# One step's order changed in the combine stage, and one product's order in the attention stage, of a two-layer decoder kernel

## The chip, the cores and the metric

The program runs on one core of one Trainium2 chip. The metric is the time of one execution on the device, in microseconds (us). Before the change it is 5105.31 us, the median of 3 runs (5102.03 to 5113.32).

## What is computed

4096 tokens, 1024 channels, in 32 blocks of 128 tokens. The reference is a decoder of two layers; cut to what matters here:

```
h   = x + pool_mixer(rmsnorm(x));  h += moe(rmsnorm(h))
h   = h + sigmoid(rmsnorm(h) @ w_ple_gate) * (p0 @ w_ple_up)
q   = rope(rmsnorm(h) @ w_q) / 8;  k = rope(rmsnorm(h) @ w_k);  v = rmsnorm(h) @ w_v
o   = attention of each 128 queries over the last 128 keys, with a sink per head
h   = h + o @ w_o;  h += moe(rmsnorm(h));  h += gated embedding p1
out = rmsnorm(h)
```

Two stages are touched. The combine stage of the first layer makes lines two and three: it adds the experts' two rows of a token, makes the gate, adds the embedding, and makes q, k and v, which it writes to HBM in the turned layout that attention reads. The attention stage makes lines four and the first half of five.

Large products are made in three bfloat16 parts: an operand is split into a high part (its bfloat16 rounding) and a low part (the rest), and high x high, high x low and low x high are summed in PSUM (`mm3`, lines 108 to 112: line 110, 111 and 112 in this order).

## The kernel before

The stages follow one another; each engine has its own instruction stream, written out by hand in a `step` function, and the streams meet at semaphores. SP issues the plain transfers and the transposing ones (`DMA_TRANSPOSE`), in program order; a wait in SP's stream holds back everything behind it.

**Combine stage** (`combine_phase`, line 1110). A step `s` works on three blocks: `head` prepares block s+1, `mid_` is the gate of block s, `tail` is q, k and v of block s-1. There are 32 blocks; step 1 is the first with a tail, step 31 the last with a gate, step 32 has the tail alone.

- TensorE (lines 1486 to 1513): 48 products with `wg` for the gate of block s (two halves of 24), then 48 with `wq` and 24 with `wkv` for block s-1. The gate reads `xT` (two buffers). The others read `x3T`, the turned third rows of block s-1, of which there is one buffer; they wait for `x3_turned`.
- VectorE (lines 1413 to 1475): h2 and the low part of x for block s+1; the residual for block s (lines 1443 and 1446) and the low part of `x3` (line 1457); then the rotation of q and k of block s-1 and the low parts of q, v and k (lines 1468, 1471, 1474). ScalarE makes the high parts (lines 1359, 1362, 1364); it writes `v_row` only when the stores of the block before have landed (`qkv_st`, line 1361).
- SP (lines 1223 to 1283), in a step with all parts: wait for `x3l_done` of block s-1 and for `kv_mm` of block s-2 (which frees `x3T`), turn `x3` into `x3T`; store q, k and v of block s-2 (`store_qkv`, which first waits for `qk_turned`); load `hin` and `p_in` of block s+2; turn `ph` and `x` of block s+1 into `pT` and `xT`; store h3 of block s, load `up_in`, store `pT`; and at the end of the step wait for `ql_done` and `kl_done` of block s-1 and turn q and k of block s-1. So x3 of block s, ready in step s, is turned at the start of step s+1, behind the turning of q and k of block s-1.

In the profile q's rows are named `cb_raw` (they share memory with a weight buffer), `x3` and `x` are both shown as `cb_x`, and all five PSUM tiles as `cb_ps_b`.

**Attention stage** (`attention_phase`, line 1762). A step `s` has eight turns c = 0 to 7, one per pair of heads. In turn c TensorE makes the scores of pair c+3 (from c = 5 on those of the next block), VectorE the masked maximum of that pair (`top`, line 2020) and the low part of the weights of pair c (`rests`, line 2037), ScalarE the exponentials (line 1961), GpSimd the high part of the weights (line 1938), and SP turns them (line 1886). Around them, on TensorE: at c = 0 and 1 the projection with `wo` of the first four pairs of block s-1, in two halves of 512 columns; at c = 2 the product of weights and values of the last four pairs (`weigh`); at c = 4 and 5 the projection of these four; at c = 6 `weigh` of the first four pairs of block s. The result of `weigh` becomes `oT`: the high part by ScalarE (`out_hi`, line 1968), the low part by VectorE (`out_lo`, line 2044). Before the projection TensorE waits for `ol_done`, the low part, at c = 0 and at c = 4. At c = 3 VectorE makes `out_lo` and then the low part of the router's rows (`hrow`, line 2088).

Of the kernel before, what the change touches and what calls it, by code (L numbers as in the profile page):

```python
# [28 lines left out]
P = 128  # L29
D = 1024  # L30
T = 4096
NT = T // P
KD = D // P
# [36 lines left out]
def wait(eng, sem, value):  # L70

    if isinstance(value, int) and value <= 0:
        return
    eng.wait_ge(sem, value)
# [1035 lines left out]
def combine_phase(nc, A, C, layer, rot):  # L1110
# [4 lines left out]
    with ExitStack() as stack:  # L1115
        m = Mem(nc, f"cb{layer}", stack)
# [15 lines left out]
        jobs += [([(A["w_q"][0], 0, D)], k, g_q, wq) for k in range(KD)]  # L1132
        jobs += [([(A["w_k"], 0, KVW), (A["w_v"], KVW, 2 * KVW)], k, g_kv, wkv) for k in range(KD)]
        GQ = KD + KD
        landed, count = [], [0] * RAW
        for n, job in enumerate(jobs):
            count[n % RAW] += 16 * len(job[0])
# [44 lines left out]
        def steps(eng, step, early=lambda: None):  # L1182

            step(-2, 0, True, False, False, False)
            early()
            step(-1, 1, True, True, False, False)
            step(0, 0, True, True, True, False)
            step(1, 1, True, True, True, True)
            with eng.Fori(1, NT // 2 - 1) as i:
                step(2 * i, 0, True, True, True, True)  # L1190
                step(2 * i + 1, 1, True, True, True, True)
            step(NT - 2, 0, False, True, True, True)
            step(NT - 1, 1, False, False, True, True)
            step(NT, 0, False, False, False, True)

        @block.sync
        def _(sp):
# [11 lines left out]
            def turn(dst, src, sem):  # L1209

                sp.dma_start(dst[:].rearrange("p h k n -> p (h k) n"), src[:].rearrange("p h d -> p (h d)"),
                             transpose=True).then_inc(sem, 16)

            def store_qkv(t):

                sp.wait_ge(qk_turned, 32 * t + 32)
                sp.sem_inc(turn_open, 1)
                at = slice(t, t + 1) if isinstance(t, int) else bass.ds(t, 1)
                for rows, src in ((C.qT_rows, q_turned), (C.kT_rows, k_turned[:].rearrange("p j n -> p (j n)")),
                                  (C.v_rows, v_row[:].rearrange("p h n -> p (h n)"))):  # L1220
                    sp.dma_start(rows[at].rearrange("o p n -> (o p) n"), src).then_inc(qkv_st, 16)

            def step(s, u, load, head, mid_, tail):
                v = 1 - u
                if tail:
                    t = s - 1
                    sp.wait_ge(x3l_done, t + 1)
                    sp.sem_inc(turn_open, 1)
                    if not (isinstance(t, int) and t == 0):
                        sp.wait_ge(kv_mm, t)  # L1230
                        sp.sem_inc(turn_open, 1)
                    turn(x3T, x3, x3_turned)
                    if not (isinstance(t, int) and t == 0):
                        store_qkv(t - 1)
                if load:
                    t = s + 2
                    wait(sp, h2_done, t - 1)
# [24 lines left out]
                if mid_:  # L1262
                    sp.wait_ge(h3_done, 2 * s + 2)
                    sp.dma_start(h3_t[s], h3[u][:]).then_inc(h3_st[u], 16)
                    if load:
# [3 lines left out]
                    at = slice(s, s + 1) if isinstance(s, int) else bass.ds(s, 1)  # L1269
                    sp.dma_start(C.pT_rows[at].rearrange("o p n -> (o p) n"),  # L1270
                                 pT[u][:].rearrange("p h k n -> p (h k n)")).then_inc(pT_st[u], 16)
                if tail:
                    t = s - 1
                    sp.wait_ge(ql_done, t + 1)
                    sp.sem_inc(turn_open, 1)
                    sp.wait_ge(kl_done, t + 1)
                    sp.sem_inc(turn_open, 1)
                    wait(sp, qkv_st, 48 * t)
                    sp.sem_inc(turn_open, 1)
                    sp.dma_start(q_turned.rearrange("p (n m) -> p n m", m=P), q_row.rearrange("p n two e -> p (n two e)"),  # L1280
                                 transpose=True).then_inc(qk_turned, 16)
                    sp.dma_start(k_turned[:], k_row[:].rearrange("p j a b e -> p (j a b e)"),
                                 transpose=True).then_inc(qk_turned, 16)

            steps(sp, step)
            store_qkv(NT - 1)
            sp.wait_ge(qkv_st, 48 * NT)
            for u in (0, 1):
                sp.wait_ge(h3_st[u], 8 * NT)
                sp.wait_ge(pT_st[u], 8 * NT)  # L1290
# [26 lines left out]
        def _(act):  # L1317
# [11 lines left out]
            def step(s, u, load, head, mid_, tail):  # L1329
# [25 lines left out]
                if tail:  # L1355
                    t = s - 1
                    act.wait_ge(rot_add, 3 * t + 2)
                    wait(act, qk_turned, 32 * t)
                    act.activation(q_row[:, :, 0, :], q_out[:].rearrange("p (n e) -> p n e", e=HEAD), ACT.Copy).then_inc(qh_done, 1)
                    act.wait_ge(rot_mul, 3 * t + 3)  # L1360
                    wait(act, qkv_st, 48 * t)
                    act.activation(v_row[:, 0, :], ps_kv[:, KVW:2 * KVW], ACT.Copy).then_inc(vh_done, 1)
                    act.wait_ge(rot_add, 3 * t + 3)
                    act.activation(k_row[:, :, 0, :, :], k_out[:].rearrange("p (j e) -> p j e", e=HEAD).unsqueeze(2).to_broadcast([P, NKV, 2, HEAD]),
                                   ACT.Copy).then_inc(kh_done, 1)
# [396 lines left out]
def attention_phase(nc, A, C):  # L1762
# [8 lines left out]
    with ExitStack() as stack:  # L1771
# [233 lines left out]
        def _(dve):  # L2005
# [53 lines left out]
            def step(s, r, load, nxt, cur, prev, prev2):  # L2059
                u = r % 2  # L2060
                v = 1 - u
                for c in range(NP):
# [11 lines left out]
                    if c == 1 and prev2:  # L2074
                        if isinstance(s, int) and s == 2:
# [2 lines left out]
                        wait(dve, hnT_mm, s - 2)  # L2078
                        dve.scalar_tensor_tensor(out=hn[:], in0=h4[u][:], scalar=rs[:, 0:1], in1=g_ffn[:],
                                                 op0=ALU.mult, op1=ALU.mult).then_inc(hn_done, 1)  # L2080
                    if c == 3 and prev:
                        out_lo(s - 1, 1)
                    if c == 4 and isinstance(s, int) and s == -1:
                        sinks()
                    if c == 3 and prev2:
                        dve.wait_ge(hi_done, s - 1)
                        dve.wait_ge(hn_done, s - 1)
                        dve.tensor_tensor(hrow[u][:, D:2 * D], hn[:], hrow[u][:, 0:D], ALU.subtract).then_inc(lo_done, 1)
                    if c in (5, 6) and prev:
                        residual(s - 1, v, c - 5)  # L2090
                    if c < NP - 3 and cur:
# [14 lines left out]
        def _(pe):  # L2106
# [27 lines left out]
                                       start=n == 0, stop=n == len(products) - 1)  # L2134
                mm.then_inc(pv_mm, 1)

            def project(n, jj):

                c = slice(512 * n, 512 * n + 512)
                for k in range(HALF * jj, HALF * jj + HALF):  # L2140
                    mm = mm3(pe, ps_x[:, c], oT[:, 0, k, :], oT[:, 1, k, :], wo[:, 0, k, c], wo[:, 1, k, c],
                             k == 0, k == KD - 1)
                return mm

            def step(s, r, load, nxt, cur, prev, prev2):
                u = r % 2
                v = 1 - u
                for c in range(NP):
                    if c < NP - 3 and cur:
                        scores(s, r, c + 3)  # L2150
                    if c == 5 and prev:
                        project(1, 1).then_inc(wo_mm, 1)
                    if c >= NP - 3 and nxt:
                        scores(s + 1, (r + 1) % KR, c + 3 - NP)
                    if c == 0 and prev:
                        if isinstance(s, int) and s == 1:
                            pe.wait_ge(w_lo_done, HALF)
                        pe.wait_ge(ol_done, 2 * s - 1)
                        wait(pe, h4_done, 2 * (s - 1))
                        project(0, 0)  # L2160
                    if c == 1 and prev:
                        project(1, 0)
                    if c == 2 and prev:
                        weigh(s - 1, (r - 1) % KR, 1)
                    if c == 3 and prev2:
# [5 lines left out]
                    if c == 4 and prev:  # L2171
                        if isinstance(s, int) and s == 1:
                            pe.wait_ge(w_lo_done, NP)
                        pe.wait_ge(ol_done, 2 * s)
                        project(0, 1).then_inc(wo_mm, 1)
                    if c == 6 and cur:
                        weigh(s, r, 0)
                    if c == 7 and prev2:
# [85 lines left out]
```

## Time and profile before

| | |
|---|---|
| median of 3 runs | 5105.31 us |
| the profiled execution | 5107.4 us, span 5105.7 us |
| TensorE matmul | 4546.8 us busy, 89% of the span |
| VectorE | 2893.9 us busy, 57% |
| ScalarE | 2044.3 us busy, 40% |
| GpSimd | 1606.1 us busy, 31% |
| TensorE clock granted, mean | 0.952 of full speed |
| combine stage, steady part | about 1680 to 2535 us of the span |
| attention stage, steady part | about 2615 to 3390 us |

Busy shares are means over the whole span; the two stages together are some 1,800 us of it. [...] A matmul of 512 columns has a record of 0.38 us at the upper level, and the next one starts 0.216 us after it; at the lower level the record has 0.63 us.

### The profile page before, as it was taken

The page shows a single profiled execution, that of the slowest core. Times are in us where ns is not written, and L with a number is a line of the kernel's source. Part 1 is how long each engine was busy: PE and PEld are TensorE (multiplying, and loading weights), DVE is VectorE, ACT ScalarE, POOL GpSimd, SP SyncE. Part 2 cuts the span into 40 slices and gives each one's busy share as a digit, 9 for nine tenths or more (in the row PEclk, how much of TensorE's full clock was granted, in tenths as well). Part 3 has the DMA queues.
Part 4 walks back from the last instruction along what each step waited for, and adds up shares of the span by engine and source line. Part 5 has one row for each costly group of instructions (what it writes and reads, how often), then busy time and mean ns, then how long its engine had stood idle before and what let it go on. Part 6 is the DMA issues. An engine that isn't in the chain of part 4 may idle for free. (4 is left out here: it accounts for less than half of the span.)

```text
span 5105.7 us, 93235 instructions
## 1 busy us (share of the span) xinstructions
PE 4546.8 (89%) x29795; PEld 2864.6 (56%) x30217; DVE 2893.9 (57%) x5879; ACT 2044.3 (40%) x2994; POOL 1606.1 (31%) x1161
## 2 busy tenths in 40 slices
PE   7986999999995899999858888886999999997999
PEld 6954776666672344444335555543676767665444
DVE  6774444444444555555468888874444444443676
ACT  6844444343432222232235454544443443331443
POOL 1104444443440111111023333422444444431332
PEclk9997999999997999999979999988999999999999
DMA  8968899898876778788677777766898889885664
GB/s 246 320 222 289 279 307 276 270 292 283 266 249 193 191 201 204 203 204 203 150 173 184 185 191 192 187 175 247 272 293 291 275 284 299 273 259 169 243 233 169
DMA packets 1262631, 1204.87 MB, mean 236 GB/s; under 512 B 925857, under 2 KB 961697, under 8 KB 1262497
## 3 DMA queue, kind: packets, MB, share of 16 engines
q1 hardware_dynamic: 1216416, 1069.05, 71.2%
q0 software_dynamic: 46080, 134.27, 8.3%
q8 instruction: 56, 0.92, 0.1%
q14 instruction: 79, 0.64, 0.0%
HBM read 742.77 MB, written 274.73 MB: 199 GB/s over the span
## 5 line engine op out<-in xcount | busy, mean ns | idle before, releaser
L837 POOL TENSOR_TENSOR ex_w_lo<-ex_raw,ex_w_hi 128x2048 bf16<-128x2048 f32 x192 | 780.6, 4090 | 1103.1 <-ACT ex_w_hi L896 1102.9
L896 ACT ACTIVATE ex_w_hi<-ex_raw 128x2048 bf16<-128x2048 f32 x384 | 707.0, 1900 | 385.8 <-PE ex_ps_y L112 189.4
L1008 PE MATMUL ex_ps_gate<-ex_xT,ex_w_hi 128*128 128x0 bf16 x2048 | 566.8, 277 | 140.1 <-DMA ex_xT<-ex_xrow 89.0
L1009 PE MATMUL ex_ps_gate<-ex_xT,ex_w_hi 128*128 128x0 bf16 x2048 | 566.7, 277 | 0.0
L1010 PE MATMUL ex_ps_gate<-ex_xT,ex_w_lo 128*128 128x0 bf16 x2048 | 566.4, 277 | 0.0
L1008 PE MATMUL ex_ps_up<-ex_xT,ex_w_hi 128*128 128x0 bf16 x2048 | 558.8, 273 | 0.0
L1009 PE MATMUL ex_ps_up<-ex_xT,ex_w_hi 128*128 128x0 bf16 x2048 | 558.6, 273 | 0.0
L1010 PE MATMUL ex_ps_up<-ex_xT,ex_w_lo 128*128 128x0 bf16 x2048 | 558.5, 273 | 0.0
L988 DVE COPY ex_y<-ex_ps_y 128x512 f32 x324 | 224.1, 692 | 566.7 <-PE ex_ps_y L112 564.4
L972 DVE TENSOR_TENSOR ex_aT<-ex_silu,ex_ps_up 128x384 bf16<-128x384 f32 x256 | 141.8, 554 | 682.8 <-PE ex_ps_up L1010 502.5
L111 PE MATMUL ex_ps_y<-ex_w_lo,ex_aT 128*128 128x512 bf16 x1296 | 492.1, 380 | 8.5
L112 PE MATMUL ex_ps_y<-ex_w_hi,ex_aT 128*128 128x512 bf16 x1296 | 491.9, 380 | 0.0
L907 ACT ACTIVATE ex_silu<-ex_ps_gate 128x384 f32<-128x384 f32 x256 | 124.8, 489 | 866.5 <-PE ex_ps_gate L1010 866.1
L1938 POOL TENSOR_TENSOR att_pr<-att_ex,att_rden 128x512 bf16<-128x512 f32 x256 | 294.1, 1149 | 489.6 <-DVE att_rden L2030 484.3
L837 DVE TENSOR_TENSOR ex_w_lo<-ex_raw,ex_w_hi 128x2048 bf16<-128x2048 f32 x192 | 439.9, 2293 | 14.3 <-ACT ex_w_hi L896 14.3
L110 PE MATMUL ex_ps_y<-ex_w_hi,ex_aT 128*128 128x512 bf16 x1134 | 431.3, 380 | 6.5 <-DVE ex_aT L976 6.5
L1961 ACT ACTIVATE att_ex<-att_score,att_nmx 128x257 f32<-128x257 f32 x512 | 256.2, 502 | 395.8 <-DVE att_nmx L2025 395.8
L111 PE MATMUL att_ps_x<-att_wo,att_oT 128*128 128x512 bf16 x512 | 218.3, 426 | 105.1 <-DVE att_oT L2044 105.1
L1008 PEld LDWEIGHTS ex_ps_gate<-ex_xT,ex_w_hi 128*128 128x128 bf16 x2048 | 203.1, 99 | 177.6 <-issue 122.5
L110 PE MATMUL cb_ps_b<-cb_wq,cb_x3T 128*128 128x512 bf16 x510 | 198.4, 389 | 79.5 <-DMA cb_x3T<-cb_x 79.4
L2020 DVE CUSTOM_DVE_ANT_0 att_score<-att_ps_s,all_mask,att_sink 128x256 f32<-128x256 f32 x496 | 218.2, 477 | 69.6 <-PE att_ps_s L2118 69.6
L110 PE MATMUL cb_ps_b<-cb_wg,cb_xT 128*128 128x512 bf16 x511 | 195.3, 382 | 60.7 <-DMA cb_xT<-cb_x 43.5
(350 smaller groups left out, 9491.2 us busy)
## 6 DMA issues: line engine op xcount, KB each, us to landing
ex_raw<-in_w_exp_gate SPq DMA_DIRECT2D x128, 1024.0 KB, 9.4
ex_raw<-in_w_exp_up SPq DMA_DIRECT2D x128, 1024.0 KB, 11.7
ex_raw<-in_w_exp_down SPq DMA_DIRECT2D x128, 1024.0 KB, 5.9
y_rows<-ex_y SPq DMA_DIRECT2D x162, 512.0 KB, 3.0
up_rows<-rt_up_out SPq DMA_DIRECT2D x64, 512.0 KB, 2.6
cb_hin<-h_mid SPq DMA_DIRECT2D x64, 512.0 KB, 3.9
cb_up_in<-up_rows SPq DMA_DIRECT2D x64, 512.0 KB, 4.5
mix_x<-in_x SPq DMA_DIRECT2D x32, 512.0 KB, 5.2
```

The lines of the kernel that those rows point to most:

```text
L110: pe.matmul(out, lhs_hi, rhs_hi, start=first, stop=False)
L111: pe.matmul(out, lhs_hi, rhs_lo, start=False, stop=False)
L112: return pe.matmul(out, lhs_lo, rhs_hi, start=False, stop=last)
L837: eng.tensor_tensor(w_lo[u][:, w], raw[:, c, :], w_hi[u][:, w], ALU.subtract).then_inc(lo_done, 1)
L896: act.activation(w_hi[u][:, c * WCHUNK:(c + 1) * WCHUNK], raw[:, c, :], ACT.Copy).then_inc(hi_done, 1)
L988: dve.tensor_copy(y[:, bass.ds(j, 1), 512 * n:512 * n + 512].rearrange("p o d -> p (o d)"), ps_y[n][:]).then_inc(y_done, 1)
L1008: pe.matmul(out, hi, x_hi, start=j == 0, stop=False)
L1009: pe.matmul(out, hi, x_lo, start=False, stop=False)
L1010: mm = pe.matmul(out, lo, x_hi, start=False, stop=j == KD - 1)
L1938: pool.tensor_tensor(pr[c % ER][:, 0, :, :], ex[c % ER][:, :, 0:W], rden[:, 2 * c:2 * c + 2].unsqueeze(2).to_broadcast([P, 2, W]), ALU.mul ...
L1961: e = act.activation(ex[c % ER][:, k, :], score[c][:, k, :], ACT.Exp, bias=nmx[:, n:n + 1], accum_out=esum[:, n:n + 1])
L2020: last = dve.tensor_tensor_reduce(out=score[c][:, k, 0:W], in0=ps_s[:, c % 2, k, :], in1=mask[:], scale=1.0, scalar=sink[:, head(c, k):hea ...
```

## The change

In the combine stage SP turns q and k of block s-2 at the start of step s, behind `x3T`, where the step before it had turned them at its end; the stores of q, k and v of block s-2 move from the start of step s to its end. `qkv_st` starts at 48, so that waits on it have positive values from the first block on. In the attention stage the projection makes all products with the high part of `oT` first, and waits for the low part only then; `out_lo` and the low part of `hrow` change places on VectorE at c = 3.

```diff
@@ combine_phase
+        QKV = 3 * 16
@@ sync
+            def turn_qk(t):
+                sp.wait_ge(ql_done, t + 1)
+                sp.sem_inc(turn_open, 1)
+                sp.wait_ge(kl_done, t + 1)
+                sp.sem_inc(turn_open, 1)
+                sp.wait_ge(qkv_st, QKV * t + QKV)
+                sp.sem_inc(turn_open, 1)
+                sp.dma_start(q_turned.rearrange("p (n m) -> p n m", m=P), q_row.rearrange("p n two e -> p (n two e)"),
+                             transpose=True).then_inc(qk_turned, 16)
+                sp.dma_start(k_turned[:], k_row[:].rearrange("p j a b e -> p (j a b e)"),
+                             transpose=True).then_inc(qk_turned, 16)
@@ step of SP
                     turn(x3T, x3, x3_turned)
                     if not (isinstance(t, int) and t == 0):
-                        store_qkv(t - 1)
+                        turn_qk(t - 1)
...
-                if tail:
-                    t = s - 1
-                    sp.wait_ge(ql_done, t + 1)
-                    sp.sem_inc(turn_open, 1)
-                    sp.wait_ge(kl_done, t + 1)
-                    sp.sem_inc(turn_open, 1)
-                    wait(sp, qkv_st, 48 * t)
-                    sp.sem_inc(turn_open, 1)
...
+                if mid_ and tail and not (isinstance(s, int) and s == 1):
+                    store_qkv(s - 2)
+
+            sp.sem_inc(qkv_st, QKV)
             steps(sp, step)
+            store_qkv(NT - 2)
+            turn_qk(NT - 1)
             store_qkv(NT - 1)
-            sp.wait_ge(qkv_st, 48 * NT)
+            sp.wait_ge(qkv_st, QKV * NT + QKV)
@@ step of ScalarE
-                    wait(act, qkv_st, 48 * t)
+                    act.wait_ge(qkv_st, QKV * t + QKV)
@@ attention_phase, step of VectorE
-                    if c == 3 and prev:
-                        out_lo(s - 1, 1)
...
                     if c == 3 and prev2:
                         dve.wait_ge(hi_done, s - 1)
                         dve.wait_ge(hn_done, s - 1)
                         dve.tensor_tensor(hrow[u][:, D:2 * D], hn[:], hrow[u][:, 0:D], ALU.subtract).then_inc(lo_done, 1)
+                    if c == 3 and prev:
+                        out_lo(s - 1, 1)
@@ TensorE
-            def project(n, jj):
+            def project(t, n, jj):
 
                 c = slice(512 * n, 512 * n + 512)
-                for k in range(HALF * jj, HALF * jj + HALF):
-                    mm = mm3(pe, ps_x[:, c], oT[:, 0, k, :], oT[:, 1, k, :], wo[:, 0, k, c], wo[:, 1, k, c],
-                             k == 0, k == KD - 1)
+                ks = range(HALF * jj, HALF * jj + HALF)
+                pe.wait_ge(oh_done, 2 * t + jj + 1)
+                for k in ks:
+                    for part in (0, 1):
+                        pe.matmul(ps_x[:, c], oT[:, 0, k, :], wo[:, part, k, c], start=k == 0 and part == 0, stop=False)
+                pe.wait_ge(ol_done, 2 * t + jj + 1)
+                for k in ks:
+                    mm = pe.matmul(ps_x[:, c], oT[:, 1, k, :], wo[:, 0, k, c], start=False, stop=k == KD - 1)
                 return mm
@@ step of TensorE
-                        pe.wait_ge(ol_done, 2 * s - 1)
                         wait(pe, h4_done, 2 * (s - 1))
-                        project(0, 0)
+                        project(s - 1, 0, 0)
...
-                        pe.wait_ge(ol_done, 2 * s)
-                        project(0, 1).then_inc(wo_mm, 1)
+                        project(s - 1, 0, 1).then_inc(wo_mm, 1)
```

## Rows read from the trace of the kernel before

**Rows 1.** Waits, whole kernel: engine line <- releaser: us, times, longest

```profile
PE att_ps_x L111 <- DVE att_oT L2044: 105.1, 63, 4.0
...
PE cb_ps_b L110 <- DMA cb_x3T<-cb_x: 79.4, 31, 11.9
```

**Rows 2.** Groups by line, PE, whole kernel: xcount | busy us, mean ns | idle

```profile
L111 PE MATMUL att_ps_x<-att_wo,att_oT 128*128 128x512 bf16 x512 | 218.3, 426 | 105.1 <-DVE att_oT L2044 105.1
...
L112 PE MATMUL cb_ps_b<-cb_wq,cb_x3T 128*128 128x512 bf16 x511 | 198.7, 389 | 1.7 <-issue 0.2
...
L110 PE MATMUL att_ps_x<-att_wo,att_oT 128*128 128x512 bf16 x448 | 188.9, 422 | 0.4 <-DVE att_oT L2044 0.4
```

**Rows 3.** Waits, PE, combine alone, 1700 to 2480 us

```profile
PE cb_ps_b L110 <- DMA cb_x3T<-cb_x: 53.8, 27, 2.4
```

**Rows 4.** Timeline, PE, combine: start us, us, line, op [idle before <-releaser]

```profile
2055.14 0.38 PE L110 MATMUL cb_ps_b<-cb_wg,cb_xT 128*128 128x512 bf16 x1
...
2065.29 0.38 PE L112 MATMUL cb_ps_b<-cb_wg,cb_xT 128*128 128x512 bf16 x1
2067.51 0.39 PE L110 MATMUL cb_ps_b<-cb_wq,cb_x3T 128*128 128x512 bf16 x1 [1.85 <-DMA cb_x3T<-cb_x]
...
2083.06 0.38 PE L110 MATMUL cb_ps_b<-cb_wg,cb_xT 128*128 128x512 bf16 x1
...
2544.81 0.61 PE L110 MATMUL cb_ps_b<-cb_wq,cb_x3T 128*128 128x512 bf16 x1 [11.91 <-DMA cb_x3T<-cb_x]
```

**Rows 5.** Timeline, SP's queue, the same combine step

```profile
2059.03 1.76 SPq L1280 DMA_TRANSPOSE cb_raw<-cb_raw  x1
...
2063.05 2.09 SPq L1211 DMA_TRANSPOSE cb_x3T<-cb_x  x1
...
2074.94 0.58 SPq L1270 DMA_DIRECT2D pT_rows<-cb_pT  x1
```

**Rows 6.** DMA issues, combine, 1700 to 2480 us: last number is us to landing

```profile
qT_rows<-cb_raw SPq DMA_DIRECT2D x27, 512.0 KB, 3.2
...
cb_x3T<-cb_x SPq DMA_TRANSPOSE x27, 4.4
```

**Rows 7.** Timeline, DVE and ACT, the same combine step

```profile
2056.28 0.38 ACT L1362 ACTIVATE cb_v_row<-cb_ps_b 128x256 bf16<-128x256 f32 x1 [2.80 <-DVE cb_rab L1400]
...
2058.08 0.68 DVE L1474 TENSOR_TENSOR cb_k_row<-cb_k_out,cb_k_row 128x512 bf16<-128x512 f32 x1
...
2071.80 1.28 DVE L1457 SCALAR_TENSOR_TENSOR cb_x<-cb_h,cb_rs,cb_x 128x1024 bf16<-128x1024 f32 x1 [1.84 <-ACT cb_x L1354]
```

**Rows 8.** Stretches, combine: us, PE, PEld, DVE, ACT, POOL busy, PEclk, DMA share

```profile
2057.00:2059.00 2.00, 2.00 (x11) 0.88 (x9) 2.00 (x4) 0.66 (x2) 0.00 (x0) 1.00 0.00 0
...
1700.00:2480.00 780.00, 722.46 (x3238) 323.27 (x3305) 436.87 (x801) 219.74 (x328) 88.69 (x134) 0.99 0.80 202
```

**Rows 9.** Timeline, PE, attention: one step's two waits, and the last step's

```profile
3050.98 0.38 PE L111 MATMUL att_ps_x<-att_wo,att_oT 128*128 128x512 bf16 x1 [0.65 <-DVE att_oT L2044]
...
3063.47 0.63 PE L111 MATMUL att_ps_x<-att_wo,att_oT 128*128 128x512 bf16 x1 [2.29 <-DVE att_oT L2044]
...
3378.11 0.38 PE L111 MATMUL att_ps_x<-att_wo,att_oT 128*128 128x512 bf16 x1 [1.39 <-DVE att_oT L2044]
```

**Rows 10.** Timeline, ACT, DVE and POOL, the same attention step

```profile
3042.34 2.00 POOL L1938 TENSOR_TENSOR att_pr<-att_ex,att_rden 128x512 bf16<-128x512 f32 x1 [0.56 <-DVE att_rden L2030]
...
3049.39 1.03 POOL L1938 TENSOR_TENSOR att_pr<-att_ex,att_rden 128x512 bf16<-128x512 f32 x1 [2.08 <-DVE att_rden L2030]
...
3061.45 0.57 ACT L1968 ACTIVATE att_oT<-att_ps_o 128x512 bf16<-128x512 f32 x1
...
3062.33 0.68 DVE L2044 TENSOR_TENSOR att_oT<-att_ps_o,att_oT 128x512 bf16<-128x512 f32 x1
```

**Rows 11.** Stretches, attention: a usual step, and one over a loop boundary

```profile
3039.65:3063.47 23.82, 20.89 (x159) 12.49 (x161) 20.49 (x74) 12.50 (x40) 9.75 (x9) 0.93 0.81 191
2790.39:2817.93 27.54, 22.53 (x159) 12.84 (x161) 21.10 (x74) 12.31 (x40) 9.75 (x9) 0.87 0.75 180
```

More of the change, by code:

```diff
@@ L1271, in step @@
                                  pT[u][:].rearrange("p h k n -> p (h k n)")).then_inc(pT_st[u], 16)
-                if tail:
-                    t = s - 1
-                    sp.wait_ge(ql_done, t + 1)
-                    sp.sem_inc(turn_open, 1)
-                    sp.wait_ge(kl_done, t + 1)
-                    sp.sem_inc(turn_open, 1)
-                    wait(sp, qkv_st, 48 * t)
-                    sp.sem_inc(turn_open, 1)
[L1280 to L1283, printed above, removed]
+                if mid_ and tail and not (isinstance(s, int) and s == 1):
+                    store_qkv(s - 2)
+            sp.sem_inc(qkv_st, QKV)
             steps(sp, step)
+            store_qkv(NT - 2)
+            turn_qk(NT - 1)
             store_qkv(NT - 1)
-            sp.wait_ge(qkv_st, 48 * NT)
+            sp.wait_ge(qkv_st, QKV * NT + QKV)
             for u in (0, 1):
@@ L2151, in step @@
                     if c == 5 and prev:
-                        project(1, 1).then_inc(wo_mm, 1)
+                        project(s - 1, 1, 1).then_inc(wo_mm, 1)
                     if c >= NP - 3 and nxt:
@@ L2157, in step @@
                             pe.wait_ge(w_lo_done, HALF)
-                        pe.wait_ge(ol_done, 2 * s - 1)
                         wait(pe, h4_done, 2 * (s - 1))
-                        project(0, 0)
+                        project(s - 1, 0, 0)
                     if c == 1 and prev:
-                        project(1, 0)
+                        project(s - 1, 1, 0)
                     if c == 2 and prev:
```

## The prediction

> **What bounds the kernel now.** I read the waits of the whole kernel first, to see whether the change touches anything that TensorE waits for. TensorE is the busiest engine, and of its waits the two largest outside the expert stage are the two that the diff is about [rows 1]: 105.1 us for the low part of `oT` in attention, 63 times, and 79.4 us for `x3T` in combine, 31 times, one of them 11.9 us long. Then the groups by line, for what a wait costs beyond itself [rows 2]: the projection's products last 426 and 422 ns on average and those with `wq` 389, where an undisturbed one lasts 380 and one at half clock 630. So some products behind the waits run at the lower clock. Last the timelines of one step of each stage.
>
> **Combine, why x3T is late.** In the steady stretch TensorE waits for `x3T` 27 times, 53.8 us together and never over 2.4 [rows 3], so 2.0 each, once per step, and for nothing else. Take the step whose gate starts at 2055.14 and call that zero; the products of k and v of the block before have just ended. The gate's last product starts at +10.15, the first `wq` product at +12.37, and the next gate at +27.92 [rows 4]. The 2.22 between the first two is one spacing of 0.216 and 2.0 of wait. SP starts turning q at +3.9, then k, and `x3T` only at +7.9 [rows 5]; with 4.4 to landing [rows 6] that is +12.3, when TensorE resumes. What SP waited for is the low part of k on VectorE, which ends at +3.6 (2058.08 + 0.68), while the low part of x3 for the next turn is ready at +17.9 (2071.80 + 1.28) [rows 7], ten microseconds before the end of the step. So x3T's rows are ready early, and stand behind q and k in SP's queue.
>
> **Combine after the change.** What must precede the turning of `x3T` is now x3 (ready at +17.9 of the step before) and the last product that reads the old `x3T`, which ends at zero. SP reacts 0.27 after its releaser (2058.76 to 2059.03), so the turning starts at about +0.3 and lands at +4.7, by 4.4 to landing [rows 6], against +10.4, when TensorE wants it: the wait goes, with 5.7 to spare. The DMA engines stand idle at about that point of the step, in the stretch from 2057 [rows 8]. q and k still go at about +3.9, since their rows aren't ready earlier: SP is done with `x3T` by then, because that instruction holds its queue some 2.1. All that follows in the queue (`hin`, `p_in`, `pT`, `xT`) moves up by about 3, having neither the 2 us of `x3T` nor the three stores in front of it, so `xT` isn't late next. The stores of q, k and v go behind the store of `pT`, which SP issues at +19.8 [rows 5] and would at about +17: they are issued by +19.5. Covered is this by the rest of the step: they must have landed before ScalarE rewrites `v_row`, which it does 1.1 after the products of k and v end [rows 7], at +27, and before q is turned at +29.8. Landing after 3.2 [rows 6] leaves 4; the cover gone, ScalarE would hold k's rows and SP, and with 10 us more the next gate. The first `sem_inc` costs nothing that can be measured.
>
> Price: the step falls from 27.9 to 25.9, the length of its 120 products. Each wait of 1.99 [rows 3] gives back 2.15, as 1.85 of shown wait went with 2.00 of gap in the step above; 30 steps, 64. The clock: `wq` products at 389 for 380 ns, out of the 250 that lie between the levels, are 4% of 1536 or 55 at half clock, 0.216 each, 12; of these I take 10, as the first and the last step keep theirs. The last tail (11.91 of wait [rows 4]) keeps 4.7 of it: 7. **Sum 81.** Bounds: 60, if a part of the waits stays, and 85.
>
> **Attention.** In a usual step TensorE waits 0.65 ahead of the last four pairs' projection and 2.29 ahead of the first four pairs' [rows 9]. Both begin in the trace with a product of line 111, where the code has line 110 first: that record is missing, so the true waits are some 0.4 and 2.0. ScalarE's high part ends at 3062.02, VectorE's low part at 3063.01 [rows 10]. Starting with the high products saves at most the 0.99 between these, and at the other place the whole 0.4. The eight high products last 1.73, longer than 0.99, so the wait for the low part is covered. At c = 3 `out_lo` now comes after a subtraction of 1024 columns, about 1.2 later at worst by the like one on x3 (1.28 [rows 7]); that too is within 1.73, and VectorE fills with it the time in which it stood waiting for ScalarE. Waits that the diff adds: one on `oh_done`, which is what the low part waited for before.
>
> The clock is the larger part. [...] By the means (424 against 380, 18% of 1536 products, 0.216 each) this costs 58 over the stage, 1.8 per step. The wait that I leave is about 1.0, nearer the two that kept the clock, and I take the whole 58. [...]
>
> TensorE alone would then need 23.82 - 1.0 - 0.4 - 1.8 = 20.6 per step, but VectorE is busy 20.49 of these 23.82 [rows 11]: from here on it binds too. The two wait for each other (VectorE for scores queued behind projections, TensorE for `oT`), so neither floor is reached; I leave VectorE 0.9 of its 3.3 idle and take 21.4. A step over a loop boundary has 27.54 [rows 11]; I give it the same 2.4. 31 steps: **75**. Bounds: 31 (1 per step, VectorE keeps most of its waits) and 99 (3.2, the floors).
>
> **A row on a port.** GpSimd's product for the weights lasts 1.03, but 2.00 where VectorE starts an operation of 1024 columns on SBUF just before it (the rows at 3049.39 and 3042.34) [rows 10]. The swap at c = 3 puts `hrow`'s subtraction in this place: right behind the reciprocal that releases GpSimd. About 2.9 of VectorE's work lies between that and its use of the product, so I price it at nothing; at worst it is 1 per step.
>
> [...]
>
> **Sum.** 81 + 75 = 156 from the profiled execution of 5107.4: 4951, which stood 2 over the median, so 4950.
>
> **Rivals.**
> 1. *The clock still falls in attention* (12%). For it: it falls after every wait of about 2.3. Against: not after 1.39. The step would be 23.82 - 1.4 = 22.4: 44 instead of 75, 4981.
> 2. *The DMA engines bind combine* (6%). They are busy 0.80 of the step [rows 8], 22.3 us, which would be 0.86 of 25.9, and the stores now fall together with h3's and the gathers. If half the gain goes: 4990. Against: a landing may be 5.7 late.
> 3. *The port* (5%): 1 per step, 31 less, 4981.
> 4. *VectorE binds attention at once* (9%): step at 22.8, 31 saved, 4994.
> 5. *The floors are reached in attention* (10%): 20.6, 99 saved, 4926.
> 6. *Slower* (3%): the stores at the step's end land late, ScalarE stands at `v_row`, and behind it k's rows, SP's turning, `xT` and the gate. It decides from landings at about +33 (6 us of slack in `xT`) and loses time in all beyond +35, as each step then waits over the 2.15 given back; at +38, 30 steps lose 3: 90 - 75 = 15 slower, 5120. Against: 3.2 to landing now.
>
> **How the numbers follow.** 55% for the forecast. The range takes in its bounds and rivals 1 to 4: 4925 to 5000. About 0.2% (10 us) is what can be told from no change. Faster 0.95; same 0.02 (combine's gain lost in part and attention's too); slower 0.03.
>
> **What would show it.** Right: no wait on `x3T` in the steady stretch, gates 25.9 apart, x3T's turning ahead of q's by some 3.6 and landing in 4 to 6; in attention steps of about 21.4, line 111's place as the waiting product taken by a high one with about 1.0, mean records of the projection near 385, VectorE over 90% busy. Wrong: a new wait on `xT`, on `v_row` or on the low part of `oT`; projection records still at 0.63; GpSimd's product at 2.00 twice a step with VectorE waiting for it.

## The result, and the profile after

The changed kernel takes 4955.36 us, the median of 4 runs (4944.96 to 4959.94), against 5106.05 of the kernel before (4 runs, 5102.03 to 5113.32): a ratio of 0.97, 95% interval 0.9682 to 0.9719, 151 us less. The forecast was 4950. The profiled execution has a span of 4954.3.

First the waits of TensorE. Below are the wait on `oT` in the whole kernel, then the groups of the products that follow it, and the group with `wq` in combine:

```profile
PE att_ps_x L2151 <- ACT att_oT L1975: 53.0, 53, 1.6
```

```profile
L2151 PE MATMUL att_ps_x<-att_wo,att_oT 128*128 128x512 bf16 x960 | 245.9, 401 | 56.9 <-ACT att_oT L1975 53.0 <-DVE att_wo L2064 3.3
...
L112 PE MATMUL cb_ps_b<-cb_wq,cb_x3T 128*128 128x512 bf16 x511 | 195.2, 382 | 1.5
...
L2154 PE MATMUL att_ps_x<-att_wo,att_oT 128*128 128x512 bf16 x512 | 136.2, 390 | 0.0
```

Against [rows 1] the wait is now for ScalarE's high part (line 1975), not for VectorE's low part, and half as long; line 2154, the products with the low part, waits for nothing. Line 2151 has 960 records where the code makes 1024 products: as in [rows 9], the record of the first product behind each of the two waits of a step is missing, and each wait is shown 0.22 too long, in all some 11 of the 53. Against [rows 2] the `wq` products are down from 389 to 382 ns, near the 380 of undisturbed ones, and the projection's from 426 and 422 to 401 and 390: not down to 380. The clock still falls in some steps.

One step of combine, on TensorE and on SP's queue:

```profile
1989.26 0.38 PE L110 MATMUL cb_ps_b<-cb_wg,cb_xT 128*128 128x512 bf16 x1
...
1999.41 0.38 PE L112 MATMUL cb_ps_b<-cb_wg,cb_xT 128*128 128x512 bf16 x1
1999.62 0.38 PE L110 MATMUL cb_ps_b<-cb_wq,cb_x3T 128*128 128x512 bf16 x1
...
2015.16 0.38 PE L110 MATMUL cb_ps_b<-cb_wg,cb_xT 128*128 128x512 bf16 x1
```

```profile
1981.82 0.33 SPq L1235 DMA_DIRECT2D v_rows<-cb_v_row  x1
1989.53 1.93 SPq L1212 DMA_TRANSPOSE cb_x3T<-cb_x  x1
1993.15 1.74 SPq L1223 DMA_TRANSPOSE cb_raw<-cb_raw  x1
...
2001.78 1.85 SPq L1212 DMA_TRANSPOSE cb_xT<-cb_x  x1
```

The gates are 25.90 apart (27.92 in [rows 4]), and the first `wq` product follows the gate's last by 0.21, one spacing. The turning of `x3T` starts 0.27 after the products that read it have ended (+7.9 in [rows 5]), that of q 3.89 after, as before. In the stretch from 1700 to 2400 us TensorE shows no wait at all.

What became of the three stores at the end of the step is seen in the DMA landings of that stretch (last number, us) and on ScalarE:

```profile
qT_rows<-cb_raw SPq DMA_DIRECT2D x27, 512.0 KB, 7.2
...
v_rows<-cb_v_row SPq DMA_DIRECT2D x27, 128.0 KB, 8.6
...
cb_x3T<-cb_x SPq DMA_TRANSPOSE x27, 4.3
```

```profile
1990.48 0.38 ACT L1369 ACTIVATE cb_v_row<-cb_ps_b 128x256 bf16<-128x256 f32 x1 [2.88 <-DMA v_rows<-cb_v_row]
```

q's store lands after 7.2 where it took 3.2 [rows 6], and v's after 8.6. The kernel before already had a store at this place in the queue, and it was as slow (1700 to 2480 us):

```profile
pT_rows<-cb_pT SPq DMA_DIRECT2D x28, 128.0 KB, 8.1
```

ScalarE now waits for that landing (64.3 us in 22 waits) in most steps, but starts 1.22 after the products of k and v end, where it started 1.14 after [rows 7].

Attention. First the stretches (columns as in [rows 11]): a usual step, one with a fallen clock, and the steady stretch of combine. Then the same usual step on its engines:

```profile
2919.72:2940.92 21.20, 19.52 (x159) 12.10 (x161) 20.45 (x74) 12.47 (x39) 10.56 (x10) 1.00 0.86 214
...
2603.72:2626.19 22.47, 21.21 (x159) 12.52 (x161) 20.48 (x74) 12.50 (x39) 10.64 (x10) 0.92 0.88 212
1700.00:2400.00 700.00, 696.42 (x3177) 317.31 (x3244) 427.36 (x786) 216.21 (x324) 87.00 (x132) 1.00 0.84 223
```

```profile
2928.66 0.57 ACT L1975 ACTIVATE att_oT<-att_ps_o 128x512 bf16<-128x512 f32 x1
...
2929.52 1.67 PE L2151 MATMUL att_ps_x<-att_wo,att_oT 128*128 128x512 bf16 x7 [0.49 <-ACT att_oT L1975]
...
2934.48 1.06 PE L2125 MATMUL att_ps_s<-att_kT,att_qT 128*128 128x128 bf16 x16
...
2935.32 0.48 DVE L2027 CUSTOM_DVE_ANT_0 att_score<-att_ps_s,all_mask,att_sink 128x256 f32<-128x256 f32 x1 [0.44 <-PE att_ps_s L2125]
...
2940.92 1.67 PE L2151 MATMUL att_ps_x<-att_wo,att_oT 128*128 128x512 bf16 x7 [1.20 <-ACT att_oT L1975]
```

A usual step has 21.20 us for 23.82, with VectorE busy in 20.45 of them: its only wait is the 0.44 for the scores that stand behind the projection. TensorE keeps two waits, shown as 1.20 at c = 0 and 0.49 at c = 4. Both groups have seven of their eight products; less 0.22 for the missing first one, the waits are 0.98 and 0.27. The run with attention alone changed (below) has all eight in its profile and shows the same wait, once with the clock fallen behind it and once not:

```profile
2905.67 3.42 PE L2144 MATMUL att_ps_x<-att_wo,att_oT 128*128 128x512 bf16 x8 [0.98 <-ACT att_oT L1968]
...
2928.12 1.89 PE L2144 MATMUL att_ps_x<-att_wo,att_oT 128*128 128x512 bf16 x8 [0.99 <-ACT att_oT L1968]
```

Taken from one router sum (line 2107) to the next, 8 of the 31 steps have 22.4, and 5 at a loop's boundary 24.9 to 27.2 (27.4 to 27.7 before). The boundary steps differ by the clock: the two of 24.9 and 25.0 ran at 1.00 and 0.99 of full speed, the three of 26.7, 26.7 and 27.2 at 0.94, 0.88 and 0.94. Two of them:

```profile
2691.50:2716.50 25.00, 19.92 (x160) 11.98 (x160) 20.70 (x73) 12.45 (x40) 10.56 (x9) 1.00 0.73 183
2781.30:2808.00 26.70, 21.49 (x159) 12.35 (x160) 20.69 (x73) 12.34 (x39) 10.56 (x9) 0.94 0.78 175
```

On GpSimd the product beside the moved subtraction has 1.85, as the row at 3042.34 in [rows 10] had 2.00:

```profile
2926.57 1.04 POOL L1945 TENSOR_TENSOR att_pr<-att_ex,att_rden 128x512 bf16<-128x512 f32 x1 [1.07 <-DVE att_rden L2037]
2928.76 1.85 POOL L1945 TENSOR_TENSOR att_pr<-att_ex,att_rden 128x512 bf16<-128x512 f32 x1 [1.16 <-DVE att_rden L2037]
```

### The profile page after: what moved, and what is told of

It reads as the page before. It is cut to its first block and busy times, and to the rows that moved or that the text cites. A ratio compares the mean times of both kernels' runs of the same rounds, so it can differ in the third digit from the quotient of the medians.

```text
span 4954.3 us, 93219 instructions
## 1 busy us (share of the span) xinstructions
PE 4502.6 (91%) x29795; PEld 2854.9 (58%) x30217; DVE 2891.0 (58%) x5879; ACT 2043.1 (41%) x2994; POOL 1631.1 (33%) x1161
## 5 line engine op out<-in xcount | busy, mean ns | idle before, releaser
L1945 POOL TENSOR_TENSOR att_pr<-att_ex,att_rden 128x512 bf16<-128x512 f32 x256 | 319.3, 1247 | 400.6 <-DVE att_rden L2037 387.8
L2151 PE MATMUL att_ps_x<-att_wo,att_oT 128*128 128x512 bf16 x960 | 245.9, 401 | 56.9 <-ACT att_oT L1975 53.0
L931 POOL DMA_INDIRECT ex_xrow<-hn_rows,ex_token x192 | 204.0, 1063 | 98.9 <-POOL ex_token L926 57.6
L2044 DVE SCALAR_TENSOR_TENSOR att_pr<-att_ex,att_rden,att_pr 128x256 bf16<-128x256 f32 x512 | 224.2, 478 | 20.2 <-issue 18.1
```

The costliest lines, as they stand in the source:

```text
L1945: pool.tensor_tensor(pr[c % ER][:, 0, :, :], ex[c % ER][:, :, 0:W], rden[:, 2 * c:2 * c + 2].unsqueeze(2).to_broadcast([P, 2, W]), ALU.mul ...
L2151: pe.matmul(ps_x[:, c], oT[:, 0, k, :], wo[:, part, k, c], start=k == 0 and part == 0, stop=False)
```

## The experiments

All are timed beside the kernel before, whose medians in the four sessions were 5104.73, 5102.48, 5103.68 and 5101.58.

**The parts by themselves.** *Combine alone*: `combine_phase` of the changed kernel, all else of the kernel before.

> Combine changed, attention as before. My account: the two parts are separate stages and add up; 82 us of the 151 are combine's (gates 25.9 apart instead of 27.9 to 30.1), so about 5024. Rival: part of the attention gain comes from combine (earlier stores, another state of clock at its start); then this gives more or less than 82 and the two parts alone don't add up to 151.

5024.96 (ratio 0.984, 0.9824 to 0.9857), 79.8 less. *Attention alone*, the other way round.

> Attention changed, combine as before. My account: 65 us less, about 5041, steps of 21.2 with some of 22.4. Rival as for the run with combine alone: the parts don't add up, and this gives under 50 or over 80.

5032.76 (0.9856, 0.9838 to 0.9874), 72.0 less. Together 151.8, against 150.7 for the changed kernel: the parts add up, and the rival (one stage lives from the other) falls. Five steps had 22.4 here, eight in the changed kernel. At 1.25 each this is 4 us, well within the 15 by which the runs of this kernel differ (5025.68 to 5040.38).

**Attention's two edits.** *Without the swap*, on the changed kernel:

```diff
@@ VectorE, c == 3
+                    if c == 3 and prev:
+                        out_lo(s - 1, 1)
...
                         dve.tensor_tensor(hrow[u][:, D:2 * D], hn[:], hrow[u][:, 0:D], ALU.subtract).then_inc(lo_done, 1)
-                    if c == 3 and prev:
-                        out_lo(s - 1, 1)
```

> The changed kernel without VectorE's swap at c = 3. My account: VectorE binds attention, and without the swap it stands about 0.5 to 0.8 us per step waiting for ScalarE's high part, so steps of 21.8 and 15 to 25 us more than the changed kernel, about 4975. Rival: the high products first carry the whole gain and the swap is worth nothing, 4955. Rival of the port: the swap costs, because the subtraction falls beside GpSimd's product; then this is faster than 4950.

4970.99 (0.9729, 0.971 to 0.9748), 16 more than the changed kernel; their runs don't overlap, by 2 us. Usual steps have 21.44, and 10 steps have about 22.5, with the clock fallen. VectorE's waits between 2620 and 3240 us:

```profile
DVE att_pr L2044 <- issue: 21.3, 5, 4.6
DVE att_oT L2051 <- ACT att_oT L1975: 20.5, 28, 0.9
DVE att_score L2027 <- PE att_ps_s L2125: 12.3, 11, 1.4
```

The wait for ScalarE's high part, 0.7 a step, is what the swap fills. Only 0.24 of it comes out at the step, since the waits for scores shrink (12.3 for 26.3 us in the same stretch of the changed kernel). In the profiles the 23 usual steps give 7 of the difference (5 by the 0.24, 2 by two falls more of the clock) and the five boundary steps 2. The rest lies outside the steps, and runs of one kernel differ by as much.

*The swap alone*, on the kernel with combine changed.

```diff
@@ VectorE, c == 3
-                    if c == 3 and prev:
-                        out_lo(s - 1, 1)
...
                         dve.tensor_tensor(hrow[u][:, D:2 * D], hn[:], hrow[u][:, 0:D], ALU.subtract).then_inc(lo_done, 1)
+                    if c == 3 and prev:
+                        out_lo(s - 1, 1)
```

> Combine changed, attention with VectorE's swap alone, the projection still waiting for the low part in one piece. My account: the low part comes up to 0.5 us later at c = 4, TensorE waits for it in full there and waits 0.65 plus that, so attention is the same or a little slower than before: 5020 to 5035, against 5024 with combine alone. Rival: VectorE's own time binds already, and filling its wait gains 10 to 20 us by itself, 5005 to 5015.

5021.43, against 5024.96 with combine alone; their runs overlap (5019.93 to 5030.31 and 5024.06 to 5028.87). The steps have 24.0 in place of 23.85, the boundary steps 26.9 (one 25.2) in place of 27.3 to 27.8. Without the high products first the swap is worth nothing that can be told: VectorE doesn't bind while TensorE waits for the whole of `oT`.

**Which move counts in combine.** *q and k turned ahead of x3T*, in the new place; the stores stay at the end.

```diff
@@ step of SP, tail
+                    if not (isinstance(t, int) and t == 0):
+                        turn_qk(t - 1)
                     sp.wait_ge(x3l_done, t + 1)
...
                     turn(x3T, x3, x3_turned)
-                    if not (isinstance(t, int) and t == 0):
-                        turn_qk(t - 1)
```

> The changed kernel, but q and k turned ahead of x3T at the start of the step; the stores stay at its end. My account: only the place of x3T ahead of the other two counts, so the wait of 2.0 per step before the products with wq comes back with its fallen clock: about 75 more than the changed kernel, 5030, gates some 27.9 apart. Rival: the gain comes from the stores having moved (they no longer stand between x3T and pT), and this keeps most of it, under 4980.

5039.97 (0.9873, 0.9854 to 0.9892), 85 more than the changed kernel: all of combine's gain is gone (with attention alone changed it was 5032.76). TensorE's wait, and SP's queue:

```profile
PE cb_ps_b L110 <- DMA cb_x3T<-cb_x: 75.1, 32, 12.0
```

```profile
2003.44 1.95 SPq L1223 DMA_TRANSPOSE cb_raw<-cb_raw  x1
2005.43 1.72 SPq L1225 DMA_TRANSPOSE cb_k_turned<-cb_k_row  x1
2007.44 1.88 SPq L1212 DMA_TRANSPOSE cb_x3T<-cb_x  x1
```

`x3T` goes 4.0 after q, as in [rows 5], and the wait is back, with the last one of 12.0. Moving the stores gives nothing by itself.

*v stored at once*, behind the turning of q and k, on a semaphore of its own.

```diff
-        QKV = 3 * 16
+        QKV = 2 * 16
...
@@ turn_qk
+                sp.dma_start(C.v_rows[at].rearrange("o p n -> (o p) n"), v_row[:].rearrange("p h n -> p (h n)")).then_inc(v_st, 16)
@@ store_qkv
-                for rows, src in ((C.qT_rows, q_turned), (C.kT_rows, k_turned[:].rearrange("p j n -> p (j n)")),
-                                  (C.v_rows, v_row[:].rearrange("p h n -> p (h n)"))):
+                for rows, src in ((C.qT_rows, q_turned), (C.kT_rows, k_turned[:].rearrange("p j n -> p (j n)"))):
...
@@ step of ScalarE
-                    act.wait_ge(qkv_st, QKV * t + QKV)
+                    wait(act, v_st, 16 * t)
```

> The changed kernel with v stored right behind the turning of q and k, on a semaphore of its own, in place of the step's end. In the changed kernel ScalarE waits 64 us in all for the landing of v. My account: that wait is off the path (TensorE has no gap at all in the steady stretch), so it vanishes from the profile and the time stays, 4950 to 4960. Rival: it is on the path in some form (it holds k's rows and so the queue); then 20 us or more go.

4960.67 (4957.73 to 4963.06; 0.9721, 0.9705 to 0.9736): no gain. ScalarE's wait for v's landing is gone from the profile:

```profile
ACT cb_v_row L1372 <- DVE cb_rab L1410: 74.4, 27, 2.8
```

It waits for VectorE instead, for as long: 74.4 us, where the changed kernel had 64.3 for the landing and 14.0 for VectorE. The 64 us cost nothing that the time shows.

**What the remaining wait costs in clock.** *Four products more* ahead of the first projection; the projection overwrites their sum.

```diff
@@ project
+                if n == 0 and jj == 0:
+                    for k in range(4):
+                        pe.matmul(ps_x[:, c], wo[:, 0, k, 0:P], wo[:, 0, k, 0:512], start=k == 0, stop=k == 3)
```

> The changed kernel with four products of 512 columns more per attention step, ahead of the first projection, whose sum the projection overwrites; they fill 0.86 of the 1.2 us in which TensorE waits there. My account: this wait makes the clock fall in about a third of the steps, which costs 1.25 each, so with it filled all steps take 21.2 and 8 to 12 us go, about 4945, though more products are made. Rival: the clock falls for the idle time in the whole step or for the place in time; then the steps of 22.4 stay and nothing is gained. Or the fill delays: 25 us slower.

4948.03 (4941.22 to 4954.46; 0.9697, 0.9682 to 0.9712). None of the 31 steps has 22.4; the usual step is 21.20 as before. The time alone would not tell it from the changed kernel, the steps do. So the falls of the clock hang on TensorE's idle time at c = 0, the 0.98. TensorE has the 0.86 of these products to spare in every step: it doesn't bind.

**Taking the wait away.** *The high part ahead of the exponentials at c = 6*:

```diff
@@ step of ScalarE
+                    if c == 6 and cur:
+                        out_hi(s, 0)
                     if c >= NP - 3 and nxt:
                         exps(s + 1, c + 3 - NP)
...
-                    if c == 6 and cur:
-                        out_hi(s, 0)
```

> The changed kernel with ScalarE's high part of oT ahead of the exponentials of pair 1 at c = 6, so that it is there before TensorE asks. My account: TensorE's wait of 1.2 goes and the clock no longer falls, but VectorE is busy 20.5 of 21.2 us and binds: steps of 20.7 to 20.9, 20 to 25 us less, about 4933. Rival: VectorE doesn't bind, the step falls by the whole wait to 20.0, 45 us less, 4910. Second rival: the exponentials come later and hold VectorE, no gain.

4944.74 (4943.22 to 4948.62; 0.9692, 0.9679 to 0.9706). The clock no longer falls in any usual step (in one boundary step, of 27.0, it does), but the step stands at 21.20, not at 20.7 to 20.9 as my account had it. TensorE's waits and VectorE's between 2600 and 3160 us:

```profile
PE att_ps_x L2151 <- ACT att_oT L1975: 28.6, 25, 1.4
```

```profile
DVE att_score L2027 <- PE att_ps_s L2125: 13.3, 26, 2.1
```

The wait went from c = 0 to c = 4, and VectorE's 0.5 for the scores behind the projection stayed. A usual wait at c = 4, with all eight products behind it:

```profile
2657.75 1.90 PE L2151 MATMUL att_ps_x<-att_wo,att_oT 128*128 128x512 bf16 x8 [1.07 <-ACT att_oT L1975]
```

These 1.07 are longer than the 0.98 at c = 0 that let the clock fall in 8 steps, and here no usual step has a fall. So the length of the wait alone does not decide whether the clock falls. What else does, no run shows. The next run does the same *at c = 2 as well*:

```diff
@@ step of ScalarE
+                    if c == 2 and prev:
+                        out_hi(s - 1, 1)
                     if c < NP - 3 and cur:
                         exps(s, c + 3)
...
-                    if c == 2 and prev:
-                        out_hi(s - 1, 1)
```

> The kernel with ScalarE's high part ahead at c = 6, and now at c = 2 as well. Both that kernel and the one with the fill stood at 21.20 per step, with TensorE's wait at c = 4 (0.5 to 1.1) and VectorE's wait of 0.5 for the scores behind the projection. My account: these two are one ring (pair 5's maximum on VectorE, its exponentials, the high part, the projection, the scores, VectorE), and with the high part ahead at c = 2 the ring opens: VectorE never waits, steps of 20.7 to 20.8, 10 to 14 us less than with c = 6 alone, about 4932. Rival: VectorE's own time is 21.2 with all that its records don't show; then nothing changes, 4945.

4934.06 (4926.69 to 4935.28; 0.9669, 0.9654 to 0.9684), with steps of 20.66. All that VectorE still waits for between 2600 and 3160 us:

```profile
DVE att_pr L2044 <- issue: 20.2, 5, 4.5
```

The five are at the loop's boundaries. So 21.20 was a ring of engines that wait for each other in turn: pair 5's maximum, its exponentials, the high part behind them on ScalarE, the two projections, the scores behind these, VectorE.

**VectorE's own time.** *The low part of hrow on GpSimd*, on the changed kernel:

```diff
@@ VectorE, ahead of hn
+                        wait(dve, lo_done, s - 2)
@@ VectorE, c == 3
-                        dve.tensor_tensor(hrow[u][:, D:2 * D], hn[:], hrow[u][:, 0:D], ALU.subtract).then_inc(lo_done, 1)
...
@@ GpSimd
+                    if c == 3 and prev2:
+                        pool.wait_ge(hi_done, s - 1)
+                        pool.tensor_tensor(hrow[u][:, D:2 * D], hn[:], hrow[u][:, 0:D], ALU.subtract).then_inc(lo_done, 1)
```

> The changed kernel with the low part of hrow made by GpSimd in place of VectorE, 1.2 us per step less on VectorE. If VectorE's time is what holds the step at 21.2: 20 to 35 us less, 4920 to 4935. If it is the ring through the high part of oT at c = 4 alone: VectorE stands 1 us longer for ScalarE or for scores and nothing is gained, 4950 to 4960. Third: GpSimd is late with the weights and holds VectorE, slower than 4960.

4964.46 (4961.94 to 4965.66; 0.9729, 0.9712 to 0.9746), 9 more than the changed kernel, with steps of 21.25: nothing is gained, and the ratios' intervals overlap. GpSimd and VectorE at that place:

```profile
2912.09 2.13 POOL L1957 TENSOR_TENSOR att_hrow<-att_hn,att_hrow 128x1024 bf16<-128x1024 f32 x1
```

```profile
2911.61 0.69 DVE L2055 TENSOR_TENSOR att_oT<-att_ps_o,att_oT 128x512 bf16<-128x512 f32 x1 [0.68 <-ACT att_oT L1979]
...
2913.14 1.11 DVE L2036 TENSOR_SCALAR att_nmx<-att_mx 128x2 f32<-128x2 f32 x1
```

VectorE loses the 1.2 again: 0.68 waiting for ScalarE, and 0.94 in an instruction of two elements per partition, the negation of a maximum. It takes 0.17 elsewhere and here ends with GpSimd's, at 2914.2. *Both high parts ahead and the rows on GpSimd*:

> Both of the above together. My account: VectorE has 19.3 of work per step, TensorE about 19.6 without waits, so steps near 20.0 and 35 to 40 us less than the changed kernel, about 4918. Rival: GpSimd's longer work takes it back, 4930 or more.

4953.53 (4943.82 to 4958.81; 0.9703, 0.9686 to 0.972), 19 worse than without the rows on GpSimd, with steps of 21.24 and no wait on VectorE but those at the boundaries. The rival holds, and its size can be read:

```profile
2728.45 2.13 POOL L1957 TENSOR_TENSOR att_hrow<-att_hn,att_hrow 128x1024 bf16<-128x1024 f32 x1
```

```profile
2728.72 1.89 DVE L2036 TENSOR_SCALAR att_nmx<-att_mx 128x2 f32<-128x2 f32 x1
```

The negation takes 1.89, 1.72 more than 0.17, and ends with GpSimd's subtraction. VectorE is freed of 1.12 (its own subtraction, to the start of what followed): 20.66 - 1.12 + 1.72 = 21.26, and the step has 21.24.

*Both high parts ahead, and the negation on ScalarE*:

```diff
@@ top, VectorE
-                dve.wait_ge(mx_done, pairs(t, c))
-                dve.tensor_scalar(nmx[:, 2 * c:2 * c + 2], mx[:, 2 * c:2 * c + 2], -1.0, None, ALU.mult).then_inc(nmx_done, 1)
@@ exps, ScalarE
+                act.wait_ge(mx_done, pairs(t, c))
+                act.activation(nmx[:, 2 * c:2 * c + 2], mx[:, 2 * c:2 * c + 2], ACT.Copy, scale=-1.0).then_inc(nmx_done, 1)
```

> The kernel with both high parts ahead, and the negation of each pair's maximum (line 2032, 2 elements, 0.17 to 0.40 us each on VectorE, 8 per step) made by ScalarE in place of VectorE. In that kernel VectorE waits for nothing and the step is 20.66, so my account: VectorE's time alone holds it; 2.0 us less on VectorE bring the step down to TensorE's 19.6 to 20.0, 20 to 30 us less, about 4908. It also takes VectorE's one instruction that stood 1.1 us behind GpSimd's long one in the run with the rows on GpSimd. Rival: ScalarE's fixed cost comes into the ring from maximum to exponentials, TensorE and VectorE wait for it, and nothing or less than 10 us is gained.

4898.82 (4896.03 to 4903.92; 0.9602, 0.9589 to 0.9615): 57 less than the changed kernel, 35 less than the one that it is built on (20 to 30 were expected), with steps of 19.75. The stretch from 2600 to 3160 us of the changed kernel, and of this one:

```profile
2600.00:3160.00 560.00, 504.93 (x3921) 304.74 (x3970) 509.29 (x1792) 310.39 (x948) 263.14 (x224) 0.97 0.85 205
```

```profile
2600.00:3160.00 560.00, 543.75 (x4371) 333.61 (x4427) 517.13 (x1773) 385.08 (x1274) 286.85 (x249) 1.00 0.97 227
```

TensorE is up from 90% to 97%, with 1.00 of the clock granted for 0.97. Of the rival's fixed cost this much is seen: ScalarE's negation of two elements has 0.20, where its exponentials of 257 columns have 0.50. This is the best version found. Its gain has two halves. The 23 usual steps give 17 us (19.75 for 20.66), and the five boundary steps another 17: they have 21.3 to 21.8 where the kernel that it is built on has 24.5 to 25.4. The stall that VectorE had there, 20.2 us in 5 above, is down to this:

```profile
DVE att_score L2029 <- issue: 0.9, 5, 0.2
```

My account was of the first half alone; why the stall goes with the negation is not shown.

## Why the prediction was right, and where not

**Combine (81; alone 80).** The step fell to the 25.9 of its products, the turning of `x3T` starts 0.27 after the reading products end and lands in 4.3, as the sum had it, and the last tail kept 4.43 of wait, where 4.7 was forecast. That the queue's order alone was at fault is shown by the run with q and k ahead, which gave all of it back.

The step that failed is "Landing after 3.2 leaves 4". That row was measured where the three stores went out behind turnings alone; behind h3, `up_in` and beside the gathers the same stores took 7.2 to 8.6, and the slack at `v_row` was not 4 but nothing. The row for the place that they were moved to was in the trace: the store of `pT` took 8.1 there. It cost nothing, as what follows it had slack of its own, which the run with v stored at once shows. This was rival 6's mechanism, short of its turning point: v's store lands at about +27, and by the prediction's own figure all is lost only beyond +35. Rival 2, the DMA engines: 0.84 busy, forecast 0.86, and no wait for them on TensorE.

**Attention (75; alone 72).** The usual step came to 21.20 for 21.4, and the wait left at c = 0 is the 1.0 of the prediction, with the missing record taken into account. But the 31 steps at 2.4 each, 75 in all, gave 63: 2.6 in 15 usual ones, 1.4 in the eight of 22.4, 0.4 to 2.7 at the boundaries, 1.6 on average in the last three. Another 5 came ahead of the first router sum (at 2583.2 us of the span, for 2587.9 with combine alone changed), where the forecast had nothing. That the total is near 75 is in part luck. In the sum itself two terms were off, in opposite directions. "I take the whole 58" of the clock: the projection's means of 401 and 390 say that 23 of 58 stayed (8% of 1024 products and 4% of 512, 0.216 each); the wait of 0.98 left it falling in 8 steps of 31 and in three boundary steps, and the run with the fill shows it by taking the 8 away. This was rival 1, in part. The two waits that the prediction says kept the clock are the 0.65 and the 1.39 of [rows 9]: the products behind them had 0.38, with 1.00 granted from 3050.98 to 3053 and from 3378.11 to 3380 us, while those behind the 2.29 had 0.63, with 0.50 granted from 3063.5 to 3065.5. The 1.39 was one step, the last, and one is too few to go by: the 0.98 of the changed kernel did let the clock fall in 8 steps, and the 1.07 at c = 4 of the run with one high part ahead, in no usual one. The mean record near 385 that was to show it came to 401 and 390. "I leave VectorE 0.9 of its idle": it kept 0.44.

"At the other place the whole 0.4" failed too: 0.27 of wait is still at c = 4, since with the rest of the step shorter ScalarE's high part, standing behind pair 5's exponentials, is not there when TensorE wants it. This was the next bound, a ring through three engines, and I had named VectorE's time instead. VectorE binds only once the ring is open: at 20.66, by the run with both high parts ahead.

**The port.** The forecast of no cost holds: the product of GpSimd has 1.85, VectorE doesn't wait for it in a usual step, and without the swap the kernel is 16 us slower. The port is the prediction's name for these overlaps of GpSimd and VectorE; no run shows what they have to do with a port. In the three read here, it is the instruction that starts second that gets longer. VectorE's subtraction of 1.20 started at 2928.51, and GpSimd's product, 0.25 later, has 1.85 for 1.03; GpSimd's subtraction of 2.13 was 1.05 and 0.27 under way in the two runs with the rows on GpSimd, and VectorE's two elements have 1.11 and 1.89 for 0.17. Where VectorE was the one held up and waited for nothing else, the step did get longer: 21.24 for 20.66. Rival 3's 1 us per step did not come about in the changed kernel, and rivals 4 and 5 fall with 21.20.

**The slower rival** and "the same" had no part in it. The steps at a loop's boundary shrank by 0.4 to 2.7, and it is the clock that sets them apart: in the changed kernel 24.9 and 25.0 without a fall, 26.7 to 27.2 with one or two. What stays open is the stall under them. In every version but the last VectorE stands there for 2.8 to 4.7 us in front of the low part of the weights (line 2037 before, 2044 after), waiting for nothing that the profile shows ("issue"). With the negations on ScalarE it does not, and no run shows why.

## What to carry to other kernels

Where one queue issues several transfers, put first the one whose data is ready and whose reader binds; the price is in the row that ends the queue's wait, not in the transfer (here `x3T` behind q and k cost 85 us, with the same transfers). A product of high and low parts can begin on the part that comes first, and the second part is then free if its delay is shorter than the products on the first (here 0.99 by [rows 10] against 1.73 for eight products, and no wait at line 2154); once this is done, look for the next engine in the ring (here ScalarE's order) before taking work off the busiest one. A small instruction on VectorE beside a long one of GpSimd can be dear: a negation of two elements took 1.89 behind a subtraction of 2.13, and undid the gain of moving that subtraction. And read what an edit gave by kinds of step: of the 35 us of the last one only half came where the account had them.

## What was not expected of the hardware

An instruction of two elements per partition on VectorE, 0.17 us by itself, took 1.11 and 1.89 when GpSimd had a 1024-column subtraction of 2.13 under way, and ended with it. Beside GpSimd's usual product of 1.03 it does so on a small scale. In a usual step of the changed kernel four of the eight negations have 0.25 to 0.40 and end within 0.04 of the product, as here:

```profile
2939.89 1.03 POOL L1945 TENSOR_TENSOR att_pr<-att_ex,att_rden 128x512 bf16<-128x512 f32 x1 [1.50 <-DVE att_rden L2037]
```

```profile
2940.56 0.40 DVE L2032 TENSOR_SCALAR att_nmx<-att_mx 128x2 f32<-128x2 f32 x1
```

All eight taken away shortened the usual step by 0.9 us; how much of this is the time held beside GpSimd, and how much the instructions themselves, was not measured apart.

The clock did not follow the length of a wait. A wait of 0.98 on TensorE at c = 0 let it fall in 8 of 31 steps of one run and in 5 of another of the same attention code, at a cost of 1.25 each, and one of 1.07 at c = 4 in no usual step. Waits of 2.0 in combine let it fall in 5 of 29 steps of the kernel before (those of 29.8 to 30.1 us), while waits of the same 2.0 in its attention stage (2.29, less the missing product) did so in every usual step.
